# One unit of weight splitting more in hand after the first norm, and a new order of the first loads

## What is computed

```python
def reference(x, ...):
    # first block: rms_norm(x, norm1_g) @ w_in gives q, three pairs of k and v,
    # three gates, conv_b, conv_c, conv_x, gate_a, gate_b
    o_nsa = g0 * o_cmp + g1 * o_slc + g2 * o_win       # three attentions, 8 heads of 64
    z = conv_b * causal_conv(conv_c * conv_x, width=3)
    x = x + (sigmoid(gate_a) * (o_nsa @ w_branch_a)
             + sigmoid(gate_b) * (z @ w_branch_b)) @ w_out
    x = x + square(relu(rms_norm(x, norm2_g) @ w_up)) @ w_down
    # second block: norm, w_in_2 gives a, gate, q, k, v, index q, k, weights, two gates
    u = conv31(a * sigmoid(gate)) + conv_b             # 31 taps
    y_conv = silu(layernorm(u)) @ w_conv_out
    y_attn = attention_on_top_64_keys(q, k, v, index) @ w_attn_out
    h = x + (g_conv * y_conv + g_attn * y_attn) @ w_mix_out
    h = h + softmax(rms_norm(h) @ wx_q, mem keys) ... @ wx_o    # cross attention, 4 heads
    h = h + square(relu(rms_norm(h) @ w_ff1)) @ w_ff2
    return rms_norm(h, norm_final_g)
```

## Time and profile before

| | |
|---|---|
| time, median of 3 runs | 935.8 us (935.45 to 936.0) |
| the profiled execution | 935.84 us |
| its span, first to last instruction | 934.0 us |
| mean granted clock of TensorE, of full speed | 0.998 |
| PE busy | 924.1 us (99%), 5515 matmuls |
| PEld busy | 795.4 us (85%) |
| DVE busy | 678.6 us (73%) |
| ACT busy | 522.4 us (56%) |
| POOL busy | 15.0 us (2%) |

### The profile page before, as it was taken

How to read it: one execution, slowest core, us unless ns; L and a number is a source line. 1 busy time by engine, 2 the same in 40 slices (tenths; PEclk the granted TensorE clock), 3 DMA queues, 4 the chain that set the end, 5 groups by cost and what they waited for, 6 DMA issues and landing times.

```text
span 934.0 us, 14398 instructions
## 1 busy us (share of the span) xinstructions
PE 924.1 (99%) x5515; PEld 795.4 (85%) x5515; DVE 678.6 (73%) x1181; ACT 522.4 (56%) x888; POOL 15.0 (2%) x20
## 2 busy tenths in 40 slices
PE   9999999999999999999999999999999999999997
PEld 7899987788888888889999988888788888888886
DVE  5769976377776666667578989998786676666665
ACT  6656677655655445555444436654946664554553
POOL 0300000000000000000000000000000000000000
PEclk9999999999999999999999999999999999999999
DMA  9854454655465656555655845555375346655551
GB/s 337 306 162 135 139 156 137 197 201 171 153 223 185 196 185 190 194 181 158 193 167 152 238 132 156 171 176 177 133 239 173 95 165 215 217 182 181 180 181 45
DMA packets 89315, 167.51 MB, mean 179 GB/s; under 512 B 7648, under 2 KB 11808, under 8 KB 89120
## 3 DMA queue, kind: packets, MB, share of 16 engines
q1 hardware_dynamic: 89024, 166.53, 55.8%
q10 hardware_dynamic: 224, 0.07, 0.0%
HBM read 163.72 MB, written 1.05 MB: 176 GB/s over the span
## 4 chain that ended last, share of the span: by engine, by line
PE 90%; DVE 4%; ACT 3%; DMA 2%; issue 1%; SPq 0%; POOL 0%; POOLq 0%; DVEq 0%; ACTq 0%
PE pb L417 87%; PE pb L421 3%; DVE YC L1895 1%; DVE wlo L1460 1%; DMA CST<-in_consts 1%; DMA raw<-in_w_in 1%; ACT whi L943 1%; ACT YC L1255 0%; ACT ZO L943 0%; ACT GA L1078 0%; DVE DG L1874 0%; SPq L360 0%; ACT L1255 0%; ACT L1078 0%; DVE GA L1755 0%
## 5 line engine op out<-in xcount | busy, mean ns | idle before, releaser
L1460 DVE TENSOR_TENSOR wlo<-raw,whi 128x1024 fp32r<-128x1024 f32 (+2 forms) x300 | 357.1, 1213 | 144.9 <-ACT whi L943 143.9
L943 ACT ACTIVATE whi<-raw 128x1024 fp32r<-128x1024 f32 (+2 forms) x302 | 309.9, 1046 | 162.7 <-PE pb L417 150.2
L417 PE MATMUL pb<-XT,whi 128*128 128x256 f32 (+1 forms) x1552 | 372.6, 323 | 0.1
L417 PE MATMUL pb<-XT,wlo 128*128 128x256 f32 (+1 forms) x1032 | 290.6, 282 | 0.0
L417 PEld LDWEIGHTS pb<-XT,whi 128*128 128x128 f32 x1552 | 257.6, 190 | 28.6 <-issue 4.3
L417 PE MATMUL pb<-whi,ZO 128*128 128x512 f32 (+1 forms) x808 | 253.1, 390 | 0.4 <-DVE wlo L1460 0.4
L417 PEld LDWEIGHTS pb<-XT,wlo 128*128 128x128 f32 (+1 forms) x1032 | 195.8, 190 | 0.5
L417 PEld LDWEIGHTS pb<-whi,ZO 128*128 128x128 f32 x808 | 151.2, 188 | 33.1 <-DVE wlo L1460 1.7
L417 PE MATMUL pb<-whi,XT 128*128 128x512 f32 (+1 forms) x544 | 176.1, 394 | 1.7 <-DVE wlo L1460 1.0
L417 PE MATMUL pb<-wlo,ZO 128*128 128x512 f32 (+1 forms) x404 | 156.5, 387 | 0.0
L417 PEld LDWEIGHTS pb<-whi,XT 128*128 128x128 f32 x544 | 101.1, 188 | 24.4 <-DVE wlo L1460 2.1
(11 more groups left out here) (226 smaller groups left out, 595.7 us busy)
## 6 DMA issues: line engine op xcount, KB each, us to landing
raw<-in_w_in SPq DMA_DIRECT2D x107, 512.0 KB, 3.8
raw<-in_w_ff SPq DMA_DIRECT2D x64, 512.0 KB, 4.4
raw<-in_w_up SPq DMA_DIRECT2D x32, 512.0 KB, 4.4
raw<-in_w_down SPq DMA_DIRECT2D x32, 512.0 KB, 4.8
raw<-in_w_branch_b SPq DMA_DIRECT2D x8, 512.0 KB, 4.4
raw<-in_w_out SPq DMA_DIRECT2D x8, 512.0 KB, 4.7
raw<-in_wx_kv SPq DMA_DIRECT2D x8, 512.0 KB, 4.4
raw<-in_w_attn_out SPq DMA_DIRECT2D x8, 512.0 KB, 3.4
```

Source lines behind the costliest of these rows:

```text
L417: return e.matmul(o, l, r, start=start, stop=stop, skip_group_check=True)
L943: return e.activation(o, i, ACT.Copy, scale=scale)
L1460: e.tensor_tensor(wlo[u % NW][:, 0:c], raw[u % NRAW][:, 0:c], whi[u % NW][:, 0:c].bitcast(F32), ALU.subtract).then_inc(lo, 1)
```

## The change

It has four parts. (1) The gain is put in front of the transposed tokens by the host, as 8 more columns of `xt` (in the packing of inputs, beside arrays that are packed there already); it comes with the first piece, and the tokens now come in four pieces. (2) The DMA on ACT's queue is no longer the gain but the first half of unit 0. (3) The high part of the first column tile is made by DVE. (4) After the squares on ACT and the factor's steps on DVE, two splits are made at once (the owed one and one more: units 7 and 8, `whi2` and `whi3`), ahead of the copies of `b1_q` and of the reduction of its heads' squares. `run("b1_kv", begin=1)` leaves out the split behind its first unit.

```diff
+        XG = work(W0 + 16232, "XG", 2056)
+        XF = XG[:, 8:2056]
...
             def load_columns(i):
-                a, b = ((0, 512), (512, 1024), (1024, 2048))[i]
-                e.dma_start(XF[:, a:b], A["xt"][:, a:b]).then_inc(xt_in[i], 16)
+                a, b = ((0, 264), (264, 520), (520, 1032), (1032, 2056))[i]
+                e.dma_start(XG[:, a:b], A["xt"][:, a:b]).then_inc(xt_in[i], 16)
 
             load_columns(0)
-            for k in range(2):
-                e.dma_start(raw[0][:, 512 * k:512 * k + 512], units[0][0][0][0][:, k, :]).then_inc(raw_in[0] if k else first_in, 16)
             load_columns(1)
+            e.dma_start(raw[0][:, 512:1024], units[0][0][0][0][:, 1, :]).then_inc(raw_in[0], 16)
+            load_columns(2)
             load(1)
-            load_columns(2)
+            load_columns(3)
             load(2)
...
-            def run(name, *sides):
+            def run(name, *sides, begin=0):
...
-                    if q < count[name] - 1:
+                    if begin <= q < count[name] - 1:
                         make_hi()
...
-            e.dma_start(PR[:, 0:8], A["params"][:, 0:8]).then_inc(gain_in, 16)
+            e.dma_start(raw[0][:, 0:512], units[0][0][0][0][:, 0, :]).then_inc(first_in, 16)
...
-            e.wait_ge(gain_in, 16)
             for j in range(4):
-                e.wait_ge(xt_in[min(j, 2)], 16)
                 for k in range(2):
                     kt = 2 * j + k
-                    copy(XT[:, kt * 512:kt * 512 + 256], XF[:, kt * 256:kt * 256 + 256], prm(GAIN[T_X], kt)).then_inc(t_hi, 1)
+                    if kt == 1:
+                        e.wait_ge(t_hi, 1)
+                    if kt:
+                        e.wait_ge(xt_in[(1, 1, 2, 2, 3, 3, 3, 3)[kt]], 16)
+                        copy(XT[:, kt * 512:kt * 512 + 256], XF[:, kt * 256:kt * 256 + 256], XG[:, kt:kt + 1]).then_inc(t_hi, 1)
...
-                run(name)
+                run(name, begin=int(n == 1))
                 for t in range(2) if n == 0 else ():
                     e.wait_ge(x_in[t], 16)
                     for i in range(2):
                         norm_square(N_X, X, i, t)
+                if n == 0:
+
+                    owed[0] = 0
+                    make_hi()
+                    make_hi()
...
+            e.wait_ge(xt_in[0], 16)
+            e.tensor_scalar(XT[:, 0:256], XF[:, 0:256], XG[:, 0:1], None, ALU.mult).then_inc(t_hi, 1)
             make_x_lo(0)
...
                 e.tensor_scalar(DR[:, t * P:t * P + P], ident, NSUM[N_X][t], None, ALU.mult).then_inc(dr_made, 1)
+            owed[0] = 0
+            make_lo()
+            make_lo()
             head_mean(0)
-            run("b1_kv")
+            run("b1_kv", begin=1)
```

More of the change, by code:

```diff
@@ L102, in build @@
         XS = work(W0 + 4096, "XS", 2048)
-        XF = work(W0 + 16240, "XF", 2048)
+        XG = work(W0 + 16232, "XG", 2056)
+        XF = XG[:, 8:2056]
         DR = work(W0 + 15224, "DR", 256)
@@ L283, in build @@
         x_in, mem_in = [sem("x_landed0"), sem("x_landed1")], [sem("mem_landed0"), sem("mem_landed1")]
-        xt_in, gain_in = [sem(f"x_columns_landed{i}") for i in range(3)], sem("first_gain_landed")
+        xt_in = [sem(f"x_columns_landed{i}") for i in range(4)]
         dr_made, rx_done, rx_out = sem("factor_diagonals"), sem("factor_rows"), sem("factor_rows_copied")
@@ L1957, in make_x_lo @@
                     e.scalar_tensor_tensor(out=XT[:, a + 256:a + 512], in0=XF[:, kt * 256:kt * 256 + 256],
-                                           scalar=prm(GAIN[T_X], kt), in1=XT[:, a:a + 256].bitcast(F32), op0=ALU.mult,
+                                           scalar=XG[:, kt:kt + 1], in1=XT[:, a:a + 256].bitcast(F32), op0=ALU.mult,
                                            op1=ALU.subtract).then_inc(t_lo, 1)
+            e.wait_ge(xt_in[0], 16)
+            e.tensor_scalar(XT[:, 0:256], XF[:, 0:256], XG[:, 0:1], None, ALU.mult).then_inc(t_hi, 1)
             make_x_lo(0)
@@ L2270 @@
     c, c2 = constants()
-    xt = I["x"].reshape(256, 8, P).transpose(2, 1, 0).reshape(P, 2048)
+    xt = np.concatenate([tiles(I["norm1_g"].reshape(-1, D)), I["x"].reshape(256, 8, P).transpose(2, 1, 0).reshape(P, 2048)],
+                        axis=1)
     arrays = {"xt": xt, "params": params, "consts": c, "consts2": c2, "wcmp": wcmp, "x": I["x"], "mem_2": I["mem_2"],
```

## The result

The changed kernel takes 949.61 us (median of 4 runs, 947.89 to 950.23) against 935.81 us before (4 runs, 935.45 to 936.0): 1.0144 times as long, 95% interval 1.0132 to 1.0157. That is 13.8 us slower. I had forecast 946.1, 10.3 slower; the time lies 0.1 us above my upper bound of 949.5. The profiled execution took 950.23 us with a span of 948.4.

What follows compares the result with a forecast made beforehand. PE was taken as the bound (90% of what ended last, busy 924.1 of 934.0 us). 935.84 - 2.0 of gains + 12.35 of costs = 946.2, predicted 946.1; range 937.5 to 949.5, 8 in 10.

Steps and rivals of the forecast that it cites:

- The start: Program start: PE begins 0.1 to 0.5 us earlier, nothing gained at the next stop; taken as 0, bounds 0 and -0.4.
- it lands at the same time: At the start: load 1 lands unchanged, with 1028 KB ahead of it over both queues before and after; 0 us.
- Units 7 and 8: Where the factor is made: early splits remove PE's 1.02 us wait at 27.89 for unit 7's low part; -1.0 us.
- UU: Products needed at 93.85: DVE 2.5 us late, less 0.56 of idle time and 0.1 of slack; +1.8 us.
- The clock: In the changed kernel's profile: clock expected at 1.00, with no term for it in the sum.
- Score pairs: Attention 1, five pairs of score blocks: each PT copy comes 0.25 to 0.35 us after it is needed; +1.55 us.
- Second attention: Conv and attention 2: split at 556.74 makes DVE 2.65 us late, with no slack at 581.11; +2.6 us.
- Cross attention: QX, behind a later-released split, is done at 725.9 while PE takes it at 724.31; +1.6 us.
- The norm: Between 664 and 676.5: weight loads' 1.7 us of waits for low parts go, 1.0 of it counted; -1.0 us.
- the side work absorbs the shift: Whole program: late side steps are caught up everywhere and only the gains remain; 933.8 us, chance 0.1.
- half: Whole program: one PE stall pays for the next, so the cost terms halve to +6.2; 940.0 us, chance 0.2.
- More than counted: Head copies, norm of the second half: three more stalls of about 1 us; 949 us, chance 0.15.

Runs made afterwards that it cites:

- The shift alone: Kernel before with one split more at b1_w's first unit, on ACT and DVE, and nothing else: 950.62 us, ratio 1.016.
- the one with three: Kernel before with units 7 and 8 early, one split more in the norm's stretch, and the new start with tokens in three pieces: 932.89 us.
- The early splits alone: Kernel before with units 7 and 8 split early, loads in the old order, later splits where they stood: 934.29 us, ratio 0.9984.
- the shift begun at b1_b0: Changed kernel, but splits stand one place earlier only from group b1_b0 on, behind the second four products UU: 946.40 us, ratio 1.0114.
- the products late: Kernel before with six idle memsets on DVE ahead of the second four products UU near 93 us: 939.19 us, ratio 1.0035.

## Why the prediction was right, and where it was off

The direction, the mechanism and every place were right: all eight costs and both gains came where they had been put, and only three others of over 0.35 us came that weren't named: the slower clock, the late load of unit 1 and the wait for a PT copy at 93.25, a sixth score pair beside the five. The shift alone costs what the changed kernel costs, and without it the 14 us are gone.

- **The start** (forecast 0): -0.73 at the first product, then +0.71 at unit 3. The step "it lands at the same time", worked out from equal bytes ahead of load 1, was 0.7 us off in this profile, some 0.6 in the mean of all, on the side that my bounds (0 to -0.4) left out; equal bytes didn't mean an equal landing, and the cause stays open. What the Trainium skill says in "DMA: Bandwidth & Descriptors", section "Issuing engines are not separate DMA queues", agrees with the traces in what it says of the loads behind: ACT's issue pulled no later load forward. None of the seven profiles with four pieces has unit 1 earlier than the kernel before, and the one with three (-0.31) lies within the spread of the old start.
- **Units 7 and 8** (-1.0): -1.37, and -0.16 at 38.49. The early splits alone gave 1.4 us, the copies that come later cost nothing.
- **UU** (+1.8): 0.39 + 1.47 = 1.86, only that the PT copy of the score pair ahead of it took a part.
- **The clock** (not in the sum): +1.46. This is the step that failed most. I summed the waits and did not ask what a wait of 1.6 us does to TensorE; "Clock 1.00" stood there without a reason. The wait of 1.02 us in the earlier trace rows had no effect on the clock, but that says nothing of a longer one.
- **Score pairs** (+1.55): +2.31. The copy is late by the whole time between PE's release and its end, 0.40 to 0.51 each; each is about 0.15 more than I read from the earlier trace rows.
- **Second UU, both FFNs, U** (+0.9, +1.4, +1.35, +1.15): 1.05, 1.49, 1.52, 1.30. Each is 0.1 to 0.17 more; no run shows why. It isn't that PE loses more than it waits: at 93.85 it waited 1.58 us and its lag grew by 1.47. The +0.9 had no working of its own (half of the first group), so that it came near is luck.
- **Second attention** (+2.6): 2.73, in two steps. **Cross attention** (+1.6): 2.08, as XT was late too (0.35).
- **The norm** (-1.0): -1.17 of the 1.7 us that PEld had waited.

The rival "the side work absorbs the shift" is refuted by the shift alone. The rival "half" is refuted by the shift begun at b1_b0 (the stalls at 93 gone, the next ones no larger) and by the shift alone (1.24 us of stall more at 38.49, the later ones no smaller). "More than counted" came nearest in the number, 949, but its places didn't come: the excess is 1.46 of clock, 0.71 at the start, 0.8 in the pairs, 0.5 in the cross attention and 0.1 to 0.2 at most other places, less 0.7 that the gains were larger than forecast. That the upper bound came as near as 0.1 us is luck: it left room for three more stalls, and those didn't come.

## What to carry to other kernels

Where splits and side work share an in-order queue and the splits run up to the buffer limit, look-ahead is not free. One more split ahead moves everything behind it by one unit of the engine that consumes, wherever there was no slack; each such place costs its lateness less its slack, and they add up. Ahead of a change of one place in such a row, compare the whole order to its end and not only the lines near the edit: an "owed" flag that is set where a step should be left out shifted over 290 splits. And a change of order can be confined: begin it where it gains and end it ahead of the first place without slack.

## What the runs showed of the hardware

After PE waits of 0.23 and 1.58 us within 2.5 us of each other, the granted clock fell from 1.00 to 0.50 some 0.5 to 1.2 us after the restart and rose again while PE was busy without a gap, in four of five profiled executions with that pair of waits; it cost 1.46 to 1.50 us. In the fifth (the shift alone) the same pair left it at 1.00, as did a single wait of 2.46 us in the profile of the products late, and waits of 1.57 us (cross attention) and 1.28 and 1.40 us (second attention) in the changed kernel's. The mean granted clocks of the executions without a profile say the same of one kernel: the changed one had the lower clock in six of eight executions (949.8 us in the mean) and not in two (948.3), and the single wait of 2.46 us brought it down in at least two of five. So such a wait costs either its length or 1.5 us more, and one profile doesn't tell which. The Trainium skill says in "TensorE: Matmul & The Clock Gate", Part 1, of a kernel's first matmuls that how many of them run at the lower clock varies from run to run. Here it is a stretch in mid-kernel that comes in some executions and not in others.
